# A two-layer trunk on one core: layer 0's MLP in two passes, adaLN sums held in PSUM

## The chip, the cores and the metric

The kernel runs on one core of one Trainium2 chip. The metric is the device time of one execution in microseconds (us). TensorE is PE below, with its weight loads as PEld; VectorE is DVE, ScalarE is ACT, GpSimd is POOL, and SyncE (SP) issues the DMAs.

## The reference

Two trunk layers run over 1024 sample tokens and 256 prompt tokens of width 1024, in float32. Both groups share the weights and differ in the conditioning vector. Cut to what matters here:

```python
def _trunk(x, cond, ...):
    for i in range(2):
        mod = (silu(cond) @ ada_w[i] + ada_b[i])[:, None, :]          # 1024 -> 6 * 1024
        sh1, sc1, g1, sh2, sc2, g2 = jnp.split(mod, 6, axis=-1)
        h = _rms_norm(x, norm_mix[i]) * (1.0 + sc1) + sh1
        if i == 0:
            out, s_new = _even_mixer(h, ...)     # w_in, gated chunks | retention, w_out
        else:
            out = _pool_mixer(h, od_w_pool, od_pool_scale)
        x = x + g1 * out
        h = _rms_norm(x, norm_mlp[i]) * (1.0 + sc2) + sh2
        x = x + g2 * (jnp.square(jax.nn.relu(h @ mlp_w1[i])) @ mlp_w2[i])   # 1024 -> 4096 -> 1024
    return _rms_norm(x, final_norm), states
```

## The kernel before, in words

**Layout and product.** Activations lie with channels on the 128 partitions and tokens along a row: X is 8 tiles of 128 channels by 1280 tokens, in three blocks of 512, 512 and 256 tokens. A float32 product is made of three fp32r matmuls: every operand is split into a high and a low part (names end in H and L), and `pair_pass` (L529) issues high by high, high by low and low by high. All weight products of the kernel have that line. Weights are loaded to `stage` by SP, 1 MB a unit, split by ACT (high, to `ringH`) and POOL (low, to `ringL`, L1520 or L1703), which hold two units.

**Stages in order.** Norms and input projections (to 484 us), retention (to about 540), out projection (24 output tiles, `out_update` on DVE adds each from its PSUM bank to X), layer 0's MLP (about 630 to 1525), the pool mixer (to about 1640), layer 1's MLP in two passes (to 2430), final norm and output.

**Layer 0's MLP.** 4096 hidden channels go in 16 chunks of 256. A chunk is the first matrix, squared ReLU, the second matrix, and the update of X (`update`, L1884, one DVE op a bank). The first chunk and the last are plain. In the other 14 (`mlp_fast`) the second matrix for the 1024 sample tokens is multiplied as a 2 x 2 of quarters with seven products in place of eight (Strassen-Winograd): 84 matmuls of 512 columns instead of 96. Its first matrix is plain: 96 of 512. The prompt's 256 tokens are plain in both: 96 of 256 columns a chunk.

**Layer 1's MLP.** Two passes. `plain_chunk` runs the first matrix of chunks 0 and 1; `first_pass` runs it for the other 14 with seven products of quarters, 84 matmuls of 512 columns and 48 of 256 a chunk. It needs sums of quarters of the normed input (G1 to G4, made on DVE ahead of the first product, L2338 to L2361), and sums of quarters of the weights (`qsF`, `qsH`, `qsL`, on POOL and ACT). Its results are combined on DVE and ACT (evictions s11, s22, s12 at L2390, squared ReLU B11, B22, B12 at L2396, sums T1 to T4 at L2372 to L2380) and stored to `mid_spill` in DRAM. `second_pass` runs the second matrix for pairs of chunks from pieces loaded back; `last_second` ends it. X is spilled and loaded again between the passes.

**adaLN sums.** ada_w is 1024 by 6144 a layer. It is loaded by SP three tiles of 128 outputs a batch, 1.5 MB, into `ada_st_in` or `ada_st_mlp`. `ada_part` on DVE (L1873, L1876) makes 16 multiply-adds of 128 x 384 for the 8 row tiles and the 2 conditionings, into `ada_acc_in` or `ada_acc_mlp` in SBUF. PE turns the sums with transposes into one PSUM bank (`ada_total`; L2780 in MLP 0), and DVE reduces them into `mod`. There are 27 batches. Eight run in the input projections, three in the out projection (`ADA_OUT_AT` says behind which of DVE's X updates the four parts of a batch stand, `OUT_TOTAL_AT` behind which output tile PE makes the total), and the 16 of layer 1 run one with each chunk of MLP 0. DVE is a queue in order: an X update behind an ada part waits for that part, and PE waits for its bank.

```python
ADA_OUT_AT = {2: (0, 0), 3: (0, 1), 4: (0, 2), 5: (0, 3), 9: (1, 0), 10: (1, 1), 11: (1, 2), 12: (1, 3),
              14: (2, 0), 15: (2, 1), 16: (2, 2), 17: (2, 3)}
OUT_TOTAL_AT = {8: 0, 14: 1, 19: 2}
```

**Between MLP 0 and the pool mixer.** Token tiles of X are transposed and normed (tH, tL), POOL builds the tables of the pooling bands (L1589 to L1616) in the last chunk of MLP 0, and the pool weights take a place in the rings.

Of the kernel before, what the change touches and what calls it, by code (L numbers as in the profile page):

```python
# [52 lines left out]
U_MLP = [U_OUT + N_OUT, U_OUT + N_OUT + 2 * NCH + 1]  # L53
U_ONE = U_MLP[1]
# [7 lines left out]
def two_units(ui, g):  # L62
# [7 lines left out]
ADA_IN_UNITS = {0: 0, 3: 1, 4: 2, 5: 3, 6: 4, 7: 5, 8: 6, 9: 7}  # L70
ADA_IN = ADA_BATCH * len(ADA_IN_UNITS)
ADA_L0 = NMOD - 2 * DT
ADA_OUT_TILES = [range(n, min(n + ADA_BATCH, ADA_L0)) for n in range(ADA_IN, ADA_L0, ADA_BATCH)]

ADA_OPS = 2 * DT
ADA_OUT_AT = {2: (0, 0), 3: (0, 1), 4: (0, 2), 5: (0, 3), 9: (1, 0), 10: (1, 1), 11: (1, 2), 12: (1, 3),
              14: (2, 0), 15: (2, 1), 16: (2, 2), 17: (2, 3)}
OUT_TOTAL_AT = {8: 0, 14: 1, 19: 2}
# [3 lines left out]
ADA_FIRST_AT = {9: 0, 12: 1, 15: 2, 18: 3}  # L82
BATCHES_IN = len(ADA_IN_UNITS)
BATCHES_L0 = BATCHES_IN + len(ADA_OUT_TILES)
# [15 lines left out]
LAST_MM_AT = {9: 0, 14: 1, 18: 2, 19: 3, 22: 4, 23: 5}  # L100
LAST_RS_AT = {11: 0, 16: 1, 19: 2, 21: 3}
LAST_LO_AT = {12: 0, 17: 1, 20: 2, 22: 3}
# [16 lines left out]
FAST = [range(1, NCH - 1), range(0)]  # L119
HD = DT // 2  # L120
FACTORS = {1: ("A11", "B11"), 2: ("A12", "B21"), 3: ("S4", "B22"), 4: ("A22", "T4"), 5: ("S1", "T1"), 6: ("S2", "T2"),
           7: ("S3", "T3")}
GOES_TO = {1: (0, 0), 2: (0, 0), 6: (0, 1), 5: (1, 1), 7: (1, 1), 3: (0, 1), 4: (1, 0)}
CHAIN = {6: 1, 7: 6, 4: 7, 3: 5}
FAST_SEQ = ([(1, d) for d in range(HD)] + [(2, d) for d in range(HD)]
            + [(p, d) for d0 in range(0, HD, 2) for p in (6, 5, 7, 3, 4) for d in (d0, d0 + 1)] + [("prompt", d) for d in range(DT)])
FAST_GRP = len(FAST_SEQ)
FAST_BANK = [(2, 3, 6, 1, 4, 5, 2, 3)[d] if p == "prompt" else (6, 1)[d % 2] if p in (2, 3, 5) else 2 + d for p, d in FAST_SEQ]
FAST_TILE = [(2, d) if p == "prompt" else (GOES_TO[p][1], HD * GOES_TO[p][0] + d) for p, d in FAST_SEQ]
FIRST_BANK = (0, 1, 0, 0, 0, 0)  # L130
LO_ORDER = ["B11", "B21", "T1", "T2", "B22", "T3", "T4", "p0", "p1"]
FAST_MID = len(LO_ORDER)


def earlier(seq, n):

    return max([i for i in range(n) if seq[i] == seq[n]], default=-1)


def products(l, ch):  # L140

    if not isinstance(ch, int):
# [104 lines left out]

END_NEED = [M2_END + DT * (1 + n // 4) for n in LAST_TILES]
# [9 lines left out]
def build(nc, ctx, x_prompt, x_sample, state_ret, c, c_ctx, ada_w, ada_b, norm_mix, norm_mlp, mlp_w1, mlp_w2,  # L258
# [13 lines left out]
    midH = at("midH", A_M, [P, HT, T], F32R)  # L272
    midL = at("midL", A_M + 10, [P, HT, T], F32R)
# [110 lines left out]
    r_b = [at(f"relu{i}", A_AD + 3 + 2 * i, [P, 512]) for i in range(3)]  # L384
# [55 lines left out]
    def sem(name, n=None):  # L440
# [37 lines left out]
    m1_mm, relu_ok, sqr_ok, mid_hi, mid_lo = (sem("m1_mm", 1), sem("relu_ok", 1), sem("sqr_ok", 1), sem("mid_hi", 1),  # L478
                                              sem("mid_lo", 1))
    m2_mm, m2_ev = sem("m2_mm", 2), sem("m2_ev", 2)  # L480

    s_add, s_hi, s_lo, t_full = sem("s_add", 1), sem("s_hi", 1), sem("s_lo", 1), sem("t_full", 1)
# [14 lines left out]
    def out_done(name, n):  # L497

        return mid_out[Q[name]], OUT_BASE[Q[name]] + 16 * n

    def in_done(name, n):

        return mid_in[Q[name]], IN_BASE[Q[name]] + 16 * n
# [29 lines left out]
    def ada_tiles(b):  # L533

        return (2 * DT + ADA_BATCH * b, ADA_BATCH) if b < BATCHES_IN else (2 * DT + ADA_OUT_TILES[b - BATCHES_IN][0],
                                                                          len(ADA_OUT_TILES[b - BATCHES_IN]))
# [33 lines left out]
    MID_PART = {"B11": (0, 0), "B21": (1, 0), "T1": (0, 1), "B22": (1, 1), "T2": (0, 0), "T3": (1, 0), "p0": (0, 2), "p1": (1, 2)}  # L570

    def hidden(name):

        if name == "T4":
            return ts4H[:, :], ts4L[:, :], r_b[0][:, :]
        k, tb = MID_PART[name]
        return tuple(m[:, k, cols(tb)] for m in (midH, midL, midF))

    def weight(l, name, d):

        if name[0] == "S":
            i = int(name[1]) - 1
            return tuple(m[:, i, d * P:(d + 1) * P] for m in (sumH, sumL))
        k, n0 = int(name[2]) - 1, HD * (int(name[1]) - 1)
        return tuple(r[(U_MLP[l] + 1) % 2][:, k * D + (n0 + d) * P:k * D + (n0 + d + 1) * P] for r in (ringH, ringL))
# [7 lines left out]
    def first_weight(slot, name, k):  # L593

        if name[0] == "S":
            i = int(name[1]) - 1
            return tuple(m[:, i, k * P:(k + 1) * P] for m in (qsH[0], qsL[0]))
        f, kk = int(name[1]) - 1, HD * (int(name[2]) - 1) + k
        return tuple(r[slot][:, kk * UC + f * P:kk * UC + (f + 1) * P] for r in (ringH, ringL))
# [6 lines left out]
    def second_weight(c, name, d):  # L606

        if name[0] == "S":
            i = int(name[1]) - 1
            return tuple(m[:, i, d * P:(d + 1) * P] for m in (qsH[c], qsL[c]))  # L610
        k, n0 = int(name[2]) - 1, HD * (int(name[1]) - 1)
        return tuple(r[(U_ONE + c) % 2][:, k * D + (n0 + d) * P:k * D + (n0 + d + 1) * P] for r in (ringH, ringL))

    def sum_full(s, i, c):

        return s4[:, :] if isinstance(s, int) and s == 0 and (i, c) == (4, 0) else qsF[c][:, i - 1, :]
# [5 lines left out]
    def slot_free(U):  # L622
# [308 lines left out]
    def _(act):  # L931
# [546 lines left out]
        for i in (1, 2):  # L1478
            sum1_hi(2, i)
# [1681 lines left out]
```

## Time and profile before

| | us |
|---|---|
| median of 3 runs (2449.01 to 2449.63) | 2449.06 |
| the profiled execution | 2447.29 |
| its span in the trace | 2445.4 |
| PE busy | 2396.3 |
| DVE busy | 1591.7 |
| POOL busy | 986.1 |
| ACT busy | 792.0 |

The span is what the trace covers; the execution's own time is 1.9 us longer, and that execution lies 1.8 us below the median. Times in the rows further down are from the start of the span. Of an engine's group of instructions the rows give the total time and, where engines are listed in order of time, the idle time before in brackets with the engine and line that ended it. The chain of waits follows the work back from the end, at each step to what released it. The granted clock (PEclk) is a share of TensorE's full clock.

### The profile page before, as it was taken

How to read it: one execution, taken by the hardware profiler on the slowest of the kernel's cores; microseconds unless marked ns; L12 is line 12 of the kernel's file. 1: busy time of each engine (PE TensorE's matmuls, PEld its weight loads, DVE VectorE, ACT ScalarE, POOL GpSimd, SP SyncE). 2: the span in 40 equal slices, each digit the busy share in tenths (PEclk: the TensorE clock that was granted, in tenths of full speed). 3: DMA queues.
4: the chain of work that ended last, by engine and by line, in shares of the span. 5: the costliest groups of instructions: out<-in, count | busy, mean ns of one | idle time of the engine just before them, and what ended most of it. 6: DMA issues, size and time to landing. Idle time of an engine off the chain costs nothing.

```text
span 2445.4 us, 37931 instructions
## 1 busy us (share of the span) xinstructions
PE 2396.3 (98%) x13516; PEld 2085.5 (85%) x13516; DVE 1591.7 (65%) x2600; ACT 792.0 (32%) x1234; POOL 986.1 (40%) x520
## 2 busy tenths in 40 slices
PE   8999999989999999999999999899999999999998
PEld 5988899988878888888888888878888888888887
DVE  6666842384588788877878876578333327877764
ACT  4321112151422232232223222764333334333322
POOL 0135311172033333333333333036656567876740
PEclk9999999999999999999999999999999999999999
DMA  8335433384122111212111221033343445343322
GB/s 295 121 130 155 138 130 113 123 290 143 57 70 69 60 60 60 103 60 77 60 60 60 73 90 36 18 121 125 109 147 105 144 174 215 133 146 120 120 86 87
DMA packets 156705, 274.07 MB, mean 112 GB/s; under 512 B 7716, under 2 KB 103752, under 8 KB 155720
## 3 DMA queue, kind: packets, MB, share of 16 engines
q1 hardware_dynamic: 149200, 263.22, 31.2%
q10 hardware_dynamic: 7416, 9.63, 1.4%
q8 instruction: 60, 0.98, 0.2%
q14 instruction: 29, 0.24, 0.0%
HBM read 204.66 MB, written 63.96 MB: 110 GB/s over the span
## 4 chain that ended last, share of the span: by engine, by line
PE 89%; DVE 6%; ACT 2%; issue 1%; DMA 1%; POOL 0%; SPq 0%; DVEq 0%; ACTq 0%; POOLq 0%
PE bank L529 84%; PE bank L2693 1%; PE bank L2581 1%; DMA hL_f<-in_ada_w_dram 1%; ACT yn L1140 1%; DVE X L1884 1%; DVE rst L2052 1%; PE bank L2780 0%; DVE G1L L2361 0%; DVE ada_acc_mlp L1876 0%; DVE xgm L2084 0%; DVE h1L L2091 0%; PE bank L2946 0%; PE bank L2640 0%; ACT pF L1190 0%
## 5 line engine op out<-in xcount | busy, mean ns | idle before, releaser
L1884 DVE SCALAR_TENSOR_TENSOR X<-bank,mod,X 128x512 f32<-128x512 f32 (+1 forms) x852 | 544.9, 683 | 233.1 <-PE bank L529 232.9
L529 PE MATMUL bank<-hH,ring 128*128 128x512 f32 (+1 forms) x2496 | 686.7, 357 | 0.6 <-DVE hL L2091 0.6
L1520 POOL TENSOR_TENSOR ring<-stage,ring 128x2048 fp32r<-128x2048 f32 x64 | 301.0, 4703 | 565.8 <-ACT ring L935 565.8
L529 PEld LDWEIGHTS bank<-hH,ring 128*128 128x128 f32 x2496 | 444.9, 189 | 66.7 <-DVE hL L2091 1.6
L529 PE MATMUL bank<-hL,ring 128*128 128x512 f32 (+1 forms) x1248 | 441.7, 354 | 0.0
L529 PEld LDWEIGHTS bank<-hL,ring 128*128 128x128 f32 x1248 | 236.1, 189 | 32.2
L529 PE MATMUL bank<-ring,hH 128*128 128x256 f32 (+1 forms) x1024 | 222.3, 313 | 0.4 <-DVE hL L1856 0.3
L935 ACT ACTIVATE ring<-stage 128x2048 fp32r<-128x2048 f32 x65 | 124.1, 1909 | 301.7 <-PE bank L529 289.8
L529 PE MATMUL bank<-midH,ring 128*128 128x256 f32 (+1 forms) x864 | 212.4, 327 | 4.3 <-DVE X L1884 4.3
L529 PE MATMUL bank<-h1H,ring 128*128 128x256 f32 (+1 forms) x864 | 209.5, 327 | 1.0 <-DVE h1L L2091 0.5
L529 PEld LDWEIGHTS bank<-ring,hH 128*128 128x128 f32 x1024 | 166.7, 190 | 11.5 <-DVE hL L1856 1.5
L2390 DVE TENSOR_TENSOR u<-u,bank 128x512 f32<-128x512 f32 x42 | 28.9, 688 | 213.8 <-PE bank L529 212.8
L529 PEld LDWEIGHTS bank<-midH,ring 128*128 128x128 f32 x864 | 147.0, 190 | 19.1 <-DVE X L1884 5.2
L529 PEld LDWEIGHTS bank<-h1H,ring 128*128 128x128 f32 x864 | 148.1, 190 | 17.2 <-DVE h1L L2091 1.8
L529 PE MATMUL bank<-ring,hL 128*128 128x256 f32 (+1 forms) x512 | 158.4, 309 | 0.0
L1876 DVE SCALAR_TENSOR_TENSOR ada_acc_mlp<-ada_st_mlp,sc,ada_acc_mlp 128x384 f32<-128x384 f32 (+1 forms) x266 | 147.8, 622 | 0.0
L1639 POOL TENSOR_TENSOR sumL<-sumF,sumH 128x2048 fp32r<-128x2048 f32 x14 | 64.7, 4621 | 204.3 <-DVE midF L2274 204.3
L529 PE MATMUL bank<-midL,ring 128*128 128x256 f32 (+1 forms) x432 | 141.2, 327 | 0.0
L529 PE MATMUL bank<-h1L,ring 128*128 128x256 f32 (+1 forms) x432 | 140.9, 326 | 0.0
L1703 POOL TENSOR_TENSOR ring<-stage,ring 128x1024 fp32r<-128x1024 f32 x32 | 85.2, 2674 | 58.5 <-ACT ring L1382 58.1
L529 PEld LDWEIGHTS bank<-ring,hL 128*128 128x128 f32 x512 | 97.4, 190 | 5.0
L1876 DVE SCALAR_TENSOR_TENSOR ada_acc_in<-ada_st_in,sc,ada_acc_in 128x384 f32<-128x384 f32 x112 | 99.6, 957 | 0.0
(382 smaller groups left out, 4833.8 us busy)
## 6 DMA issues: line engine op xcount, KB each, us to landing
stage<-in_mlp_w_dram SPq DMA_DIRECT2D x64, 1024.0 KB, 5.5
ada_st_mlp<-in_ada_w_dram SPq DMA_DIRECT2D x18, 1536.0 KB, 8.3
stage<-in_ev_w_in_dram SPq DMA_DIRECT2D x14, 1024.0 KB, 6.0
mid_spill<-midT SPq DMA_DIRECT2D x56, 256.0 KB, 2.2
ada_st_in<-in_ada_w_dram SPq DMA_DIRECT2D x8, 1536.0 KB, 8.3
mid_spill<-midB SPq DMA_DIRECT2D x48, 256.0 KB, 2.0
gt<-gate_spill SPq DMA_DIRECT2D x20, 256.0 KB, 3.8
x_spill<-X SPq DMA_DIRECT2D x2, 2560.0 KB, 10.5
```

The lines of the kernel that those rows point to most:

```text
L529: mm = nc.tensor.matmul(out, a, b, start=first and n == 0, stop=last and n == 2, skip_group_check=chained)
L935: nc.scalar.activation(ringH[slot][:, :], stage[:, :], ACT.Copy).then_inc(w_hi, 1)
L1140: ev = nc.scalar.activation(yn[n % 2][:, d, h, :], bank[2 + 2 * (n % 2) + d][:, h * P:(h + 1) * P], ACT.Identity, scale=rmv[n % 2][:, j, 1 ...
L1520: nc.gpsimd.tensor_tensor(ringL[slot][:, :], stage[:, :], ringH[slot][:, :].bitcast(F32), ALU.subtract).then_inc(w_lo, 1)
L1639: nc.gpsimd.tensor_tensor(sumL[:, :, :], sumF[:, :, :], sumH[:, :, :].bitcast(F32), ALU.subtract).then_inc(s_lo[l], 1)
L1703: nc.gpsimd.tensor_tensor(rows_of(ringL[slot], part), rows_of(stages[c], part), rows_of(ringH[slot], part).bitcast(F32), ALU.subtract).the ...
L1876: V.scalar_tensor_tensor(out=acc, in0=src, scalar=sc2[:, k, cond:cond + 1], in1=acc, op0=ALU.mult, op1=ALU.add).then_inc(a_acc, 1)
L1884: V.scalar_tensor_tensor(out=X[:, d, cols(t)], in0=src[:, 0:TB[t][1]], scalar=gate_ap, in1=X[:, d, cols(t)], op0=ALU.mult, op1=ALU.add).th ...
L2052: e = V.bn_stats(rst[n % 2][:, HEADS * d + h, :], bank[2 + 2 * (n % 2) + d][:, h * P:(h + 1) * P])
L2390: V.tensor_tensor(buf[:, :], buf[:, :], src[:, :], ALU.add).then_inc(m_dve, 1)
L2581: mm = nc.tensor.matmul(bank[6 + d][:, h * P:(h + 1) * P], kx[j % 2][:, d, h, :], val[:, n, h * P:(h + 1) * P], start=True, stop=True)
L2693: mm = nc.tensor.transpose(tile_pair(q, j)[:, d * P:(d + 1) * P], X[:, d, n * P:(n + 1) * P], ident)
```

## The change: MLP 0 takes the form of MLP 1, and the adaLN batches move

- **MLP 0** becomes the same code as MLP 1 (`mlp(l)` on each engine): two plain chunks, 14 first-pass chunks with seven products, `mid_spill` stores, X spilled and loaded again, seven second passes and `last_second`, whose banks are `CLOSE_BANK` for layer 0. It needs the G quarters of its input, as layer 1. The weight-quarter buffers of layer 0 lie in free parts of other tiles.
- **Layer 1's adaLN** sums: 14 of the 16 batches run one with each first-pass chunk of MLP 0. Each is loaded in two halves of 768 KB (`ada_chunk_load`, behind the stores of B11 and B21 on SP's queue), added up by DVE in two halves of 8 ops (`ada_half`) with the running sums in two PSUM banks (`chunk_bank`); only the last op of each conditioning writes SBUF (`chunk_acc`). PE turns them behind product 2 (`ada_chunk_turn`, 6 transposes) and DVE reduces them behind B11 (`ada_chunk_columns`). For the last chunk the second half falls between the passes.
- **The other two batches**, six tiles, go into the projections: nine batches in the input projections (an additional `ada_batch(1)` behind the statistics of the gates' norm), four in the out projection, in two parts each, with totals behind tiles 4, 8, 12 and 17. The loads keep their place on SP's queue.
- **The end of MLP 0**: ada work is gone from it; `LAST_MM_AT`, the order of the last token tiles, moves by a step; POOL builds the band tables behind MLP 0's last w2 low parts; the pool weights have buffers of their own (wpH, wpL), and the token tiles lie in scattered places.

```diff
-ADA_IN_UNITS = {0: 0, 3: 1, 4: 2, 5: 3, 6: 4, 7: 5, 8: 6, 9: 7}
+ADA_IN_UNITS = {0: 0, 1: 1, 3: 2, 4: 3, 5: 4, 6: 5, 7: 6, 8: 7, 9: 8}
-ADA_OUT_AT = {2: (0, 0), 3: (0, 1), 4: (0, 2), 5: (0, 3), 9: (1, 0), 10: (1, 1), 11: (1, 2), 12: (1, 3),
-OUT_TOTAL_AT = {8: 0, 14: 1, 19: 2}
+ADA_OUT_AT = {1: (0, 0), 2: (0, 1), 5: (1, 0), 6: (1, 1), 9: (2, 0), 10: (2, 1), 13: (3, 0), 14: (3, 1)}
+OUT_TOTAL_AT = {4: 0, 8: 1, 12: 2, 17: 3}
-LAST_MM_AT = {9: 0, 14: 1, 18: 2, 19: 3, 22: 4, 23: 5}
+LAST_MM_AT = {9: 0, 14: 1, 18: 2, 19: 3, 21: 4, 23: 5}
+CLOSE_BANK = [LAST_BANK[i % 4] for i in range(GRP - 4)] + [2, 3, 4, 5]
+ADA_CHUNKS = NCH - PLAIN
...
+    def chunk_bank(cond):
+
+        return (ADA_BANK, ROW_BANK)[cond][:, 0:ADA_BATCH * P]
...
+        def ada_half(n, half):
+
+            done = ADA_OPS * (BATCHES_BEFORE + n)
+            dve.wait_ge(a_raw, 16 * (BATCHES_BEFORE + 1) + 32 * n + 16 * half)
+            if half == 0:
+                dve.wait_ge(a_col, 2 * BATCHES_BEFORE + n)
+            for i in range(DT * half, DT * (half + 1)):
+                k, cond = divmod(i, 2)
+                sums = chunk_bank(cond).rearrange("p (j n) -> p j n", j=ADA_BATCH)
+                src = chunk_st[:, k - HD * half, :].rearrange("p (j n) -> p j n", j=ADA_BATCH)
+                if k == 0:
+                    V.tensor_scalar(sums, src, sc2[:, k, cond:cond + 1], None, ALU.mult).then_inc(a_acc, 1)
+                else:
+                    dve.wait_ge(a_acc, done + i - 1)
+                    V.scalar_tensor_tensor(out=sums if k < DT - 1 else chunk_acc[:, cond, :, :], in0=src, scalar=sc2[:, k, cond:cond + 1],
+                                           in1=sums, op0=ALU.mult, op1=ALU.add).then_inc(a_acc, 1)
...
+        def ada_chunk_turn(n):
+
+            pe.wait_ge(a_acc, ADA_OPS * (BATCHES_BEFORE + n) + ADA_OPS)
+            pe.wait_ge(mod_ok, 3)
+            for cond in range(2):
+                for j in range(ADA_BATCH):
+                    mm = nc.tensor.transpose(chunk_bank(cond)[:, j * P:(j + 1) * P], chunk_acc[:, cond, j, :], ident)
             mm.then_inc(a_mm, 1)
...
-        mlp(0, 0, first=True)
-        with pe.Fori(1, NCH - 1) as ch:
-            mlp_fast(0, ch)
-        mlp(0, NCH - 1, last=True)
...
+        mlp(0)
```

## Rows read from the trace of the kernel before

**Rows 1.** The page, busy time of each engine.

```profile
PE 2396.3 (98%) x13516; PEld 2085.5 (85%) x13516; DVE 1591.7 (65%) x2600; ACT 792.0 (32%) x1234; POOL 986.1 (40%) x520
```

**Rows 2.** The page, the chain that ended last, by line.

```profile
PE bank L529 84%; PE bank L2693 1%; PE bank L2581 1%; DMA hL_f<-in_ada_w_dram 1%; ACT yn L1140 1%; DVE X L1884 1%; DVE rst L2052 1%; PE bank L2780 0%; DVE G1L L2361 0%; DVE ada_acc_mlp L1876 0%; DVE xgm L2084 0%; DVE h1L L2091 0%; PE bank L2946 0%; PE bank L2640 0%; ACT pF L1190 0%
```

**Rows 3.** The chain in MLP 0: start, length, work.

```profile
888.87 46.95 PE bank L529 x252
...
941.97 46.95 PE bank L529 x252
```

**Rows 4.** The chain in layer 1's MLP and at its end.

```profile
1684.60 337.14 PE bank L529 x1800
...
2029.28 372.15 PE bank L529 x1956
2402.30 5.46 PE bank L529 x24
...
2421.34 2.87 PE bank L529 x24
```

**Rows 5.** DVE in order of time, one first-pass chunk of layer 1.

```profile
1801.01 0.69 DVE L2390 TENSOR_TENSOR u<-u,bank 128x512 f32<-128x512 f32 x1 [6.24 <-PE bank L529]
1801.73 1.81 DVE L2396 SCALAR_TENSOR_TENSOR u<-u 128x512 f32<-128x512 f32 x1
...
1817.51 0.69 DVE L2390 TENSOR_TENSOR u<-u,bank 128x512 f32<-128x512 f32 x1 [9.64 <-PE bank L529]
1818.23 1.38 DVE L2396 SCALAR_TENSOR_TENSOR midB<-u 128x512 f32<-128x512 f32 x1
1825.85 0.69 DVE L2390 TENSOR_TENSOR u<-u,bank 128x512 f32<-128x512 f32 x1 [6.23 <-PE bank L529]
```

**Rows 6.** DVE and POOL in order of time, out projection.

```profile
563.01 1.14 DVE L1873 TENSOR_SCALAR ada_acc_mlp<-ada_st_mlp,sc 128x384 f32<-128x384 f32 x2 [2.70 <-DMA ada_st_mlp<-in_ada_w_dram]
...
565.78 2.20 DVE L1876 SCALAR_TENSOR_TENSOR ada_acc_mlp<-ada_st_mlp,sc,ada_acc_mlp 128x384 f32<-128x384 f32 x4
...
602.60 3.61 DVE L1876 SCALAR_TENSOR_TENSOR ada_acc_mlp<-ada_st_mlp,sc,ada_acc_mlp 128x384 f32<-128x384 f32 x4
598.53 5.68 POOL L1520 TENSOR_TENSOR ring<-stage,ring 128x2048 fp32r<-128x2048 f32 x1 [21.06 <-ACT ring L935]
```

**Rows 7.** The page, DMA issues: KB each, us to landing.

```profile
ada_st_mlp<-in_ada_w_dram SPq DMA_DIRECT2D x18, 1536.0 KB, 8.3
```

**Rows 8.** DVE in order of time, input projections.

```profile
123.54 0.40 DVE L1964 RECIPROCAL vmv<-vmv 128x40 f32<-128x40 f32 x1 [12.02 <-ACT vmv L1107]
```

**Rows 9.** SP's queue in order of time, start of the out projection.

```profile
546.89 5.24 SPq L668 DMA_DIRECT2D ada_st_mlp<-in_ada_w_dram  x1
```

**Rows 10.** The chain in the out projection.

```profile
556.98 27.57 PE bank L529 x144
```

**Rows 11.** Windows: length, busy PE PEld DVE ACT POOL, clock, DMA share, GB/s.

```profile
1540.00:1544.00 4.00, 3.58 (x18) 3.56 (x18) 1.24 (x4) 3.67 (x8) 1.12 (x2) 0.57 0.00 0
```

**Rows 12.** Waits of PE: 630 to 730, 1630 to 1690, 1690 to 2060, 1488 to 1532.

```profile
PE bank L529 <- DVE X L1884: 2.1, 2, 1.7
...
PE bank L529 <- DVE G4L L2361: 1.9, 1, 1.9
PE bank L529 <- DVE h1L L2091: 0.5, 1, 0.5
...
PE bank L529 <- POOL ring L1703: 2.1, 1, 2.1
...
PE bank L529 <- DVE X L1884: 2.3, 1, 2.3
```

**Rows 13.** POOL in order of time: band tables, w2 low parts of layer 1.

```profile
1476.60 0.70 POOL L1589 MEMSET bandT<- 128x144 f32 x4
...
1488.75 0.10 POOL L1616 MEMSET band_edge<- 128x1 f32 x1
...
2375.40 6.36 POOL L1703 TENSOR_TENSOR ring<-stage,ring 128x1024 fp32r<-128x1024 f32 x2 [26.44 <-ACT ring L1382]
```

More of the change, by code:

```diff
@@ L568, in h_part, with tile_half, tile_rows, held_rows @@
         return (hH, hL)[part][:, d, cols(tb)]
[L570 to L585, printed above, removed]
+    def tile_half(part, n, d):
+        w = TILE_ROW[n]
+        return tile_at[n][part][:, d * P // w, d * P % w:d * P % w + P]
+    def tile_rows(n, ap):
+        return ap[:, :].rearrange("p (r w) -> p r w", w=TILE_ROW[n])
+    def held_rows(l, name, ap):
+        return ap.rearrange("p (a n) -> p a n", a=2) if l == 0 and name in ("T3", "T4") else ap
+    def held_part(l, name, m, c):
+        return m[l][name][:, 2 * c:2 * c + 2, :] if l == 0 and name in ("T3", "T4") else m[l][name][:, c, :]
+    def chunk_bank(cond):
+        return (ADA_BANK, ROW_BANK)[cond][:, 0:ADA_BATCH * P]
     def mid_at(s, name, c=None):
@@ L1305, in _ @@
+        mlp(0)
+        act.wait_ge(w_raw, raw_at(U_POOL, 1))
+        act.wait_ge(q_lo, Q_ALL)
+        nc.scalar.activation(wpH[:, :], stage[:, :], ACT.Copy).then_inc(w_hi, 1)
         act.wait_ge(band_ok, 1)
@@ L1496, in _ @@
[L1496 to L1507 removed]
+        mlp(1)
         for j in range(NT):
@@ L1774, in _ @@
[L1774 to L1781 removed]
+        mlp(1)
     @block.vector
@@ L2309, in _ @@
+        mlp(0)
+        for i, (t, d) in enumerate(BY_END):
+            update(m2_mm[0], M2_END + i + 1, m2_ev[0], bank[CLOSE_BANK[i]], mod[:, 0, 5 * DT + d, TB[t][2]:TB[t][2] + 1], t, d,
+                   (m2_ev[0], M2_END))
+            if i == 15:
+                pool_mods()
+            if i in LAST_LO_AT:
+                pool_tile_lo(LAST_LO_AT[i])
+            if i in LAST_RS_AT:
+                pool_rs(LAST_RS_AT[i])
+        pool_rs(5)
+        pool_tile_lo(5)
         for n in range(4):
@@ L2456, in _ @@
-        mid_low(0, "T2")
-        second_pass(0)
-        with dve.Fori(1, NSUP - 2) as s:
-            second_pass(s)
-        second_pass(NSUP - 2, plain=True)
-        mid_low(NSUP - 1, "T1", 3)
-        mid_low(NSUP - 1, "B22", 4)
+        mlp(1)
         for i, (t, d) in enumerate(BY_LAST):
@@ L2475, in ada_total @@
             after(pe, a_col, 2 * batch)
-            _, tiles = ada_tiles(batch)
+            _, _, tiles = ada_tiles(batch)
             for cond in range(2):
```

1829 lines of the change are left out of this document (779 added, 1050 removed).

## The prediction

> **What bounds the kernel now.** I read the page first. Its busy line [rows 1] has PE at 98% of the span, DVE at 65%; the chain [rows 2] is PE for 89%, nearly all of it the three-pass product of L529. So a time goes down here by taking matmuls away, or up by making PE wait. Next the chain inside layer 0's MLP: one fast chunk of 256 hidden channels is an unbroken run of products, from 888.87 to 941.97, 53.1 us [rows 3]. The chain in layer 1's MLP, which already runs in two passes, is one run of 1800 matmuls in the first pass and one of 1956 in the second [rows 4], 24.84 us from one s12 eviction on DVE to the next in the first pass [rows 5].
>
> The ends of the run in layer 1 give the price of a matmul: 24 of 512 columns took 5.46 us (0.2275 each), 24 of 256 took 2.87 (0.1196 each) [rows 4]. Check: a layer-0 fast chunk issues 180 of 512 (96 in the first matrix, 84 in the second), 96 of 256 and 6 transposes. The run of 252 matmuls took 46.95 us [rows 3] and the 24 left 5.46, so the transposes have 53.10 - 46.95 - 5.46 = 0.7: 180 x 0.2275 + 96 x 0.1196 + 0.7 = 53.1, as measured. A layer-1 first-pass chunk issues 84 and 48: 19.1 + 5.7 = 24.85, as measured.
>
> **The product work (removed).** Layer 0's first matrix goes from plain to seven products of quarters in 14 chunks: 12 matmuls of 512 columns fewer in each, 168 in all. 168 x 0.2275 = 38.2 us. The second matrix, the two plain chunks and all transposes keep their number (27 batches before and after). The check against rows, where two passes of the form of layer 1's stand for the new chunk: 53.10 - 0.7 - 2 x 24.84 = 2.7 a chunk, 38 in all. Term: **-38.2**.
>
> **Its cover on DVE.** PE's work only counts if DVE, ACT and POOL keep pace. In layer 1's first pass DVE is idle 6.24 and 9.64 us a chunk before its evictions [rows 5]; its own work is s12 and B12 (0.69 + 1.81) and s22 and B22 (0.69 + 1.38) as shown there, and six ops more (s11, B11, four T sums), 0.69 each like the undisturbed ones: 8.7 us, 8.8 with gaps. In layer 0 come two reduces (0.55 each) and 16 multiply-adds of 128x384. Their sums now lie in PSUM. No row shows DVE writing PSUM. Bounds: from below 0.53 us, the spacing of the SBUF form (2.20 for four [rows 6], the last of them overlapped for 0.08 by the next op); from above 1.81 us, the op with two SBUF inputs beside a busy POOL [rows 5]. I take 0.55, since the eviction that reads a bank took 0.69 for 512 columns whether its neighbour was slowed or not [rows 5], and the ada ops that slowed (3.61 for four, from 602.60, while a POOL sum ran from 598.53 to 604.21 [rows 6]) had both inputs in SBUF, which the new form has not. Sum: 8.8 + 1.1 + 16 x 0.55 = 18.7 of 24.85 us. Hidden; cost 0. It is cover no longer above (24.85 - 9.9) / 16 = 0.93 us an op. The Trainium skill (SBUF — State Buffer, "Who interferes with whom") says that a DVE instruction with at most one SBUF input doesn't contend with GpSimd; the rows above agree, and by that rule this term is 0 as well. The Trainium skill (VectorE: DVE Perf Modes, "The TRN2 errata") charges a PSUM source 62 cycles of 0.96 GHz more than an SBUF one, 65 ns; by it, as an estimate, 16 ops would take 1.0 us more a chunk, still inside the idle time, while no row here shows the difference.
>
> Placement in a chunk, T0 = the s12 eviction: first half 8.1 to 12.4, in the 9.64 us idle, so s22 isn't late; then SP issues the second 768 KB (1.5 MB land in 8.3 us [rows 7], so half in 4 to 5), which has landed at 17.5; second half 18.7 to 23.3, behind s22 and B22; s12 is due at 24.85. Queued behind this wait on DVE is only s12, with 1.5 us to spare, and PE needs its bank only a product later. SP's stage load has some 2.6 us of slack. Cost 0, up to 1 us a chunk if the load is late.
>
> **Six tiles into the projections.** In the input projections one batch more runs after bn_stats, where DVE is idle 12.02 us [rows 8] before 40 normalisations: 8.7 us fit. Cost 0; 0 to 1.
>
> In the out projection four batches run for three, and the first total goes from after output tile 8 to after tile 4. That is where I find a stall. SP's first load is issued at 546.89, behind the reload of X [rows 9], and DVE waits for it until 563.01 [rows 6]. Then 16 ops (0.53 apart) and one X update (0.66) behind the first eight: 9.2, ready at 572.2. PE reaches the new total after tile 4: tiles 3 (512 columns) and 4 (256) lie ahead from 556.98 [rows 10], 5.46 + 2.87, so 565.3. PE stands 6.9 us; behind the waiting transposes on PE are all later tiles. Before, the total stood at 556.98 + 27.57 = 584.55, so nothing waited. Later totals fit within 0 to 2 us: the second batch is loaded from 573, lands about 584 and is done at about 592, where tile 8 then ends. I take 0.5. Terms: **+6.9**, **+0.5**. The load isn't moved ahead of X's reload, so nothing excludes this; a gap between 4 (load lands sooner because fewer spills precede it) and 9 is the bound.
>
> After a gap PE's clock falls. In the pool stage, behind gaps of PE, the mean granted clock was 0.57 from 1540 to 1544 [rows 11], most of it at the lower level, 1.2 GHz. Work that would take (1 - 0.57) x 4 = 1.7 us at 2.4 GHz is lost: **+1.7** (0 to 3.4). The Trainium skill (TensorE: Matmul & The Clock Gate, Part 1) says that idleness takes the array to 1.2 GHz until activity releases it; the rows agree.
>
> **The start of MLP 0.** Before, PE waited 2.1 us for X updates behind ada ops [rows 12]. The ada ops go, and with them this wait; the norms' own waits stay. But the seven-product form needs G quarters before its first product, as in layer 1, where PE waited 1.9 for G4L and 0.5 for h1L [rows 12]; one more us, an estimate, for the last batch's two reduces ahead of them: 3.4 against 2.1. **+1.3** (-1 to +6).
>
> **Between the passes.** Layer 1 waits 2.1 us for the POOL ring [rows 12]. Layer 0 has there also the last ada half, whose load is behind the reload of X while all DMA engines are busy; DVE would end it about 2.4 us behind the product that wants its evictions. Total **+2.5** (2 to 8).
>
> **The end of MLP 0.** Before: 3.8 us without work on PE, 2.3 of them for an X update stuck behind ada ops [rows 12]. After: no ada ops there; about 1 us for w2's low parts (POOL took 6.36 us for two of them after the same point in layer 1 [rows 13]) and the tail, 1.5 before for token tiles, shorter by 0.8 at least: 3.8 to 0.8 in all. The band tables, about 12.3 us on POOL from 1476.60 [rows 13], now run behind them, ending 19.8 us after the last full pass while PE wants them at 23.3: hidden, 3.5 us of slack. **-3.0** (-4 to +3).
>
> Sum: -38.2 + 6.9 + 0.5 + 1.7 + 1.3 + 2.5 - 3.0 = -28.3. The profiled execution took 2447.29 (span 2445.4), so 2419.0 by its own time; the median of the runs is 2449.06, 1.8 higher, so **2420.8 us**, a ratio of 0.988.
>
> **Rivals.**
> A, **DVE becomes the bound** in layer 0's first pass, the case on the other side. Mechanism: the multiply-add on PSUM costs more than the SBUF form or still slows beside POOL. From 0.93 us an op each chunk lengthens by 16 times the excess; the gain of 28.3 is gone at 2.02 us a chunk, (24.85 + 2.02 - 9.9) / 16 = 1.06 us an op. At 0.90 (the four beside POOL) it is still hidden; at 1.2 us it gives 14 x 4.3 = 60 us more, 2480. For it: slow ops of DVE in [rows 5, 6] are real. Against: each has two SBUF inputs.
> B, **the out projection doesn't stall**: the load lands early, or the wait is absorbed by the queue of X updates. Then -28.3 - 6.9 - 1.7: 2412. For it: the idle of DVE before 563.01 was only 2.70 us; against: even without that idle the ops end at 569.5, 4 us late.
> C, **the seams cost more**: at the transition and at the last batch the ada load, X's reload and the spills share the DMA engines, or the band tables or low parts come late. Upper bounds above: +5.5, +4.7 and +6, not all at once: 2430 to 2437.
> D, **the first pass leaks a little**: late second halves, 1 us a chunk, 14 in all: 2435. DVE then is late for s12, shown as a wait of PE in each chunk.
>
> **Numbers.** Forecast 0.60; B 0.14; C 0.11; D 0.07; A 0.08, of which 0.02 ends between 2430 and 2444, 0.01 near no change, 0.05 above. A measurement of this kernel tells 0.2%, 4.9 us, from no change. Faster by more than that: 0.60 + 0.14 + 0.11 + 0.07 + 0.02 less 0.03 for mishaps I haven't named = 0.91; same 0.02; slower 0.07. The range must reach B below and most of C and D above: 2408 to 2436. It leaves out the worst of C, A, and a product work that is worth more than counted. The seams' bounds, B's 4 to 9 us, and the clock's 0 to 3.4 are inside.
>
> **What would show it.** Matmuls of 512 columns fewer by 168 and PE busy lower by about 38 us; fast chunks in layer 0's first pass of 24.8 to 25.2 us; no wait of PE there; the multiply-adds on PSUM at 0.53 to 0.6 us each, whatever POOL does. In the out projection a wait of PE for the ada sums near 565, of about 7 us, with a lower clock behind it. PE idle of 2 to 3 us between layer 0's passes. Against me: chunks of 26 us or more with PE waiting for DVE (A, D); no wait near 565 (B); the sum of PE's idle time from 1400 to 1500 over 5 us (C).

## The result, and the profile after

The changed kernel took 2421.93 us, median of 4 runs (2420.18 to 2423.78), where the kernel before took 2449.35 in the runs beside it: a ratio of 0.9887, 95% interval 0.987 to 0.9904. The forecast was 2420.8, a ratio of 0.988. By the profiled executions the span went from 2445.4 to 2419.0, 26.4 us less, where 28.3 were forecast.

The page of the changed kernel, busy time of each engine, answers to [rows 1]:

```profile
PE 2362.3 (98%) x13348; PEld 2057.9 (85%) x13348; DVE 1546.0 (64%) x2313; ACT 836.4 (35%) x1299; POOL 1203.2 (50%) x702
```

PE has 168 instructions fewer (13516 to 13348), exactly the matmuls counted, and is busy 34.0 us less. POOL has 217 us more work (the weight-quarter sums of a second MLP), and PE waits for it in the new stage only at the end, 0.9 us. PE's idle time rose from 49.1 to 56.7 us: 7.6 more, where the waits among the prediction's terms add up to 8.2 (6.9 + 0.5 + 1.3 + 2.5 - 3.0).

The chain of waits of the changed kernel in layer 0's first pass; columns as in [rows 3]. A chunk is 24.87 us of products and 0.66 of transposes, 25.53 in all:

```profile
792.02 0.66 PE bank L2634 x6
792.68 24.87 PE bank L529 x132
817.55 0.66 PE bank L2634 x6
818.21 24.87 PE bank L529 x132
```

DVE in such a chunk, with one op of POOL in it: the multiply-adds with their sums in PSUM run beside POOL's work. L2187 at 888.81 and 914.34 is the eviction s12 of two chunks in a row, L2095 begins a batch's first half, and the L2098 group at 908.03 begins its second:

```profile
882.51 3.23 DVE L2098 SCALAR_TENSOR_TENSOR bank<-chunk_st,sc,bank 128x384 f32<-128x384 f32 x6
883.70 3.79 POOL L1561 TENSOR_TENSOR hL<-hL_f,hH 128x512 fp32r<-128x512 f32 x3
888.81 0.69 DVE L2187 TENSOR_TENSOR u<-u,bank 128x512 f32<-128x512 f32 x1 [2.03 <-PE bank L529]
...
896.71 1.14 DVE L2095 TENSOR_SCALAR bank<-chunk_st,sc 128x384 f32<-128x384 f32 x2
...
908.03 3.23 DVE L2098 SCALAR_TENSOR_TENSOR bank<-chunk_st,sc,bank 128x384 f32<-128x384 f32 x6
...
914.34 0.69 DVE L2187 TENSOR_TENSOR u<-u,bank 128x512 f32<-128x512 f32 x1 [2.03 <-PE bank L529]
```

What PE waited for in the changed kernel, whole span (total, times, longest), the rows with adaLN and layer 0's seams in them:

```profile
PE bank L2334 <- DVE ada_acc_mlp L1787: 6.8, 1, 6.8
...
PE bank L529 <- POOL ring L1598: 3.0, 2, 2.1
...
PE bank L2634 <- DVE chunk_acc L2098: 2.3, 1, 2.3
...
PE bank L529 <- ACT u L1253: 1.7, 1, 1.7
```

The first is the stall in the out projection, forecast at 6.9. The third is the seam between layer 0's passes, forecast at 2.5. Of the second, 2.1 are layer 1's, as in [rows 12], and 0.9 are w2's low parts at the end of MLP 0, forecast at 1. The fourth lies in the first of the first-pass chunks, and no term had it. The chain there shows ACT splitting the last G quarter just before it evicts the bank that PE wants:

```profile
740.59 1.85 ACT G4H L1244 x4
...
743.45 0.58 ACT u L1253
```

The chain around the stall shows how it is made: the reload of X ahead in SP's queue (L791), the landing of the batch, and DVE's ops, then PE's transposes at 574.04, where the products before them ended at 567.2:

```profile
541.80 6.23 SPq L791
548.03 0.05 issue
548.12 16.64 DMA ada_st_mlp<-in_ada_w_dram
564.79 1.13 DVE ada_acc_mlp L1784 x2
```

And the clock behind it, windows of the changed kernel (length, busy time of PE, PEld, DVE, ACT, POOL with instructions, granted clock, DMA share, GB/s):

```profile
574.00:576.00 2.00, 1.96 (x9) 1.96 (x10) 1.04 (x2) 0.00 (x0) 0.00 (x0) 0.50 0.23 46
576.00:578.00 2.00, 2.00 (x12) 2.00 (x11) 0.00 (x0) 0.00 (x0) 0.00 (x0) 0.50 0.91 339
578.00:580.00 2.00, 2.00 (x14) 2.00 (x14) 0.00 (x0) 0.00 (x0) 0.00 (x0) 0.74 1.03 386
```

At a clock of 0.50, that is 1.2 GHz, then 0.74: 2 x 0.5 + 2 x 0.5 + 2 x 0.26 = 2.5 us of work lost, where 1.7 were forecast. The second execution of the changed kernel lost 1.7 behind the same wait, and the six variants that kept the stall 1.7 to 2.7.

### The profile page after: what moved, and what is told of

It is laid out like the page before. It is cut to its first block, busy times and chain, and to the rows that moved or that the text cites. A ratio compares the mean times of both kernels' runs of the same rounds, so it can differ in the third digit from the quotient of the medians.

```text
span 2419.0 us, 37354 instructions
## 1 busy us (share of the span) xinstructions
PE 2362.3 (98%) x13348; PEld 2057.9 (85%) x13348; DVE 1546.0 (64%) x2313; ACT 836.4 (35%) x1299; POOL 1203.2 (50%) x702
## 4 chain that ended last, share of the span: by engine, by line
PE 86%; DVE 8%; ACT 2%; DMA 1%; issue 1%; SPq 1%; POOL 0%; DVEq 0%; ACTq 0%; POOLq 0%
PE bank L529 81%; PE bank L2548 1%; DVE G1L L2158 1%; SPq L678 1%; DMA ada_st_mlp<-in_ada_w_dram 1%; PE bank L2436 1%; DMA hH_f<-in_ada_w_dram 1%; DVE G1F L2135 1%; DVE rst L1964 1%; ACT yn L1147 1%; PE bank L2844 0%; DVE G3F L2138 0%; DVE xgm L1996 0%; POOL ring L1598 0%; PE bank L2634 0%
## 5 line engine op out<-in xcount | busy, mean ns | idle before, releaser
L529 PE MATMUL bank<-hH,ring 128*128 128x256 f32 (+1 forms) x2856 | 634.4, 332 | 2.1 <-POOL ring L1598 0.9
L1795 DVE SCALAR_TENSOR_TENSOR X<-bank,mod,X 128x512 f32<-128x512 f32 (+1 forms) x576 | 373.4, 686 | 267.4 <-PE bank L529 266.1
L1447 POOL TENSOR_TENSOR ring<-stage,ring 128x2048 fp32r<-128x2048 f32 x47 | 224.6, 4778 | 295.4 <-ACT ring L942 295.4
L2187 DVE TENSOR_TENSOR u<-u,bank 128x512 f32<-128x512 f32 x84 | 57.8, 688 | 304.9 <-PE bank L529 303.0
L1598 POOL TENSOR_TENSOR ring<-stage,ring 128x1024 fp32r<-128x1024 f32 x64 | 165.2, 2597 | 112.4 <-ACT ring L1264 111.8
L529 PEld LDWEIGHTS bank<-ring,hH 128*128 128x128 f32 x1024 | 166.7, 190 | 12.2 <-DVE hL L1767 1.5
L1264 ACT ACTIVATE ring<-stage 128x1024 fp32r<-128x1024 f32 x64 | 65.8, 1056 | 219.4 <-DMA stage<-in_mlp_w_dram 181.4
L1618 POOL TENSOR_TENSOR qsL<-qsF,qsH 128x512 fp32r<-128x512 f32 x83 | 126.9, 1553 | 0.0
L1253 ACT ACTIVATE u<-bank 128x512 f32<-128x512 f32 x84 | 50.3, 599 | 196.6 <-PE bank L529 196.6
L942 ACT ACTIVATE ring<-stage 128x2048 fp32r<-128x2048 f32 x48 | 91.7, 1910 | 75.2 <-PE bank L529 71.4
L1610 POOL TENSOR_TENSOR qsF<-stage 128x512 f32<-128x512 f32 x42 | 78.3, 1876 | 56.6 <-PE bank L529 56.6
L529 PE MATMUL bank<-inpH,ring 128*128 128x256 f32 x512 | 94.5, 284 | 0.0
```

The costliest lines, as they stand in the source:

```text
L529: mm = nc.tensor.matmul(out, a, b, start=first and n == 0, stop=last and n == 2, skip_group_check=chained)
L942: nc.scalar.activation(ringH[slot][:, :], stage[:, :], ACT.Copy).then_inc(w_hi, 1)
L1253: nc.scalar.activation(dst[:, :], src[:, :], ACT.Copy).then_inc(m_act, 1)
L1264: nc.scalar.activation(rows_of(ringH[(U_MLP[l] + c) % 2], part), rows_of(stages[c], part), ACT.Copy).then_inc(w_hi, 1)
L1447: nc.gpsimd.tensor_tensor(ringL[slot][:, :], stage[:, :], ringH[slot][:, :].bitcast(F32), ALU.subtract).then_inc(w_lo, 1)
L1598: nc.gpsimd.tensor_tensor(rows_of(ringL[slot], part), rows_of(stages[c], part), rows_of(ringH[slot], part).bitcast(F32), ALU.subtract).the ...
```

## The experiments

Each starts from the changed kernel unless its edit says otherwise. Runs with several rounds are compared by their medians with its 2421.93.

**The out projection without its stall.**

```diff
-ADA_OUT_AT = {1: (0, 0), 2: (0, 1), 5: (1, 0), 6: (1, 1), 9: (2, 0), 10: (2, 1), 13: (3, 0), 14: (3, 1)}
-OUT_TOTAL_AT = {4: 0, 8: 1, 12: 2, 17: 3}
+ADA_OUT_AT = {1: (0, 0), 2: (0, 1), 7: (1, 0), 8: (1, 1), 11: (2, 0), 12: (2, 1), 15: (3, 0), 16: (3, 1)}
+OUT_TOTAL_AT = {6: 0, 10: 1, 14: 2, 19: 3}
```

> The changed kernel with its out projection's later adaLN batches and totals moved back: totals behind output tiles 6, 10, 14 and 19 in place of 4, 8, 12 and 17, and the DVE parts of batches 1 to 3 behind X updates 7/8, 11/12 and 15/16. Theory: the 6.8 us wait of PE for the ada sums near 567 goes, because DVE ends them at 574 and PE is then in tile 6, and with it the 2.5 us of half clock behind it: 9.3 us less, 2412.6 us for a kernel of 2421.9. Rival 1: the wait only moves to a later total, since the load of the next batch starts no earlier: then 0 to 4 us less. Rival 2: the half clock had another cause than this gap: then 6.8 less, and the clock near 575 is still about 0.5.

2413.79 us (2413.26 to 2414.45), ratio to before 0.9852 (0.9836 to 0.9869), 8.1 less than the changed kernel, where 9.3 were expected. The chain in this stretch of the out projection is products and transposes with nothing between them:

```profile
559.91 14.84 PE bank L529 x88
574.75 0.66 PE bank L2334 x6
575.41 19.22 PE bank L529 x96
```

The window of this kernel from 570 to 580 has PE busy throughout and the granted clock at 1.00:

```profile
570.00:580.00 10.00, 10.00 (x48) 8.32 (x48) 5.34 (x10) 1.92 (x1) 5.22 (x1) 1.00 0.47 165
```

Stall and half clock went together, and neither rival held: no later total waits. By the spans of the profiled executions the gain is 6.4: against the 9.3 taken away stand 1.3 us more of waits for pF in the pool stage (4.8 against 3.5) and 1.7 us of clock at 1650 to 1655, in layer 1's MLP.

**PE repeats 12 matmuls a chunk.**

```diff
-                    for k in range(HD):
+                    for k in [0, 1, 2, 3] * (2 if l == 0 and w_name == "A12" else 1):
```

> The changed kernel with the product A12 by B21 of layer 0's 14 first-pass chunks issued twice into its bank (the second pass of it sums on: the output of these chunks isn't the reference's): 12 matmuls of 512 columns more in each, as many as the seven-product form took away. Theory: PE is the bound in this stage with nothing to spare beside it, so the time goes up by 168 x 0.2275 = 38.2 us, to 2460.1. Rival: something else paces part of these chunks (DVE, the loads), so that matmuls there are partly free: less than 34 us.

2459.98 us (2457.38 to 2463.61), 38.05 more, against 38.2. The chain shows a chunk's products at 27.59 us where they were 24.87, which is 38.1 us in 14 chunks:

```profile
769.29 27.59 PE bank L529 x144
```

168 matmuls cost their full price in this stage, so the ones that the change removed were worth what was counted.

**The sums in SBUF.**

```diff
-                sums = chunk_bank(cond).rearrange("p (j n) -> p j n", j=ADA_BATCH)
+                sums = chunk_acc[:, cond, :, :]
```

> The changed kernel with the running ada sums of layer 0's first pass in SBUF (chunk_acc) in place of PSUM, so each multiply-add has two SBUF inputs; all else as it is. Theory: beside POOL's sums these ops slow down, as the sum u<-u does (1.8 for 0.7 us): the 8 of the second half take 6 to 9 us in place of 4.3, and the 8 of the first half 5 to 7; DVE's work goes from 18.3 to 22 to 26 us of the chunk's 25.5, so PE begins to wait or just doesn't: 2422 to 2450 us. Rival A (PSUM as the place of the sums is worth nothing here): the ops stay at 0.54 us each and the time at 2422.

2489.59 us (2482.53 to 2494.48), 67.7 more; ratio to before 1.0166 (1.0139 to 1.0192). Against before the whole change is then a loss. The changed kernel's DVE, groups of instructions from 744 to 1060 (busy us, mean ns):

```profile
L2098 DVE SCALAR_TENSOR_TENSOR bank<-chunk_st,sc,bank 128x384 f32<-128x384 f32 x150 | 80.9, 611 | 4.0 <-DMA chunk_st<-in_ada_w_dram 4.0
```

The groups with the sums in SBUF, from 770 to 1070 (the first and the third are those of the adaLN sums):

```profile
L2098 DVE SCALAR_TENSOR_TENSOR chunk_acc<-chunk_st,sc,chunk_acc 128x384 f32<-128x384 f32 x147 | 157.6, 1140 | 34.7 <-DMA chunk_st<-in_ada_w_dram 34.7
L2187 DVE TENSOR_TENSOR u<-u,bank 128x512 f32<-128x512 f32 x32 | 21.7, 677 | 0.0
L2095 DVE TENSOR_SCALAR chunk_acc<-chunk_st,sc 128x384 f32<-128x384 f32 x20 | 20.3, 1057 | 1.1
```

The multiply-add went from 611 to 1140 ns in the mean (lengths of single records, which overlap: on PSUM the next one starts after 0.525). DVE's eviction, which reads a bank, stayed at 677, and DVE is never idle before it: it was late each time. DVE in order of time shows the slowing, first in an op with one SBUF input and an SBUF output (the median of the 28 of its kind is 0.42 us), then in six multiply-adds; eight others took less:

```profile
895.67 4.77 DVE L2095 TENSOR_SCALAR chunk_acc<-chunk_st,sc 128x384 f32<-128x384 f32 x1
900.36 8.33 DVE L2098 SCALAR_TENSOR_TENSOR chunk_acc<-chunk_st,sc,chunk_acc 128x384 f32<-128x384 f32 x6
...
914.21 5.36 DVE L2098 SCALAR_TENSOR_TENSOR chunk_acc<-chunk_st,sc,chunk_acc 128x384 f32<-128x384 f32 x8 [4.19 <-DMA chunk_st<-in_ada_w_dram]
```

POOL in order of time has one op of the same length over the first, was busy beside the six up to 907.75, and was idle from there to 917.36:

```profile
895.48 4.75 POOL L1447 TENSOR_TENSOR ring<-stage,ring 128x2048 fp32r<-128x2048 f32 x1
...
903.11 4.64 POOL L1561 TENSOR_TENSOR hL<-hL_f,hH 128x512 fp32r<-128x512 f32 x3
...
917.36 1.79 POOL L1561 TENSOR_TENSOR hL<-s,hH 128x512 fp32r<-128x512 f32 x1 [9.61 <-ACT hH L1249]
```

The direction was as expected and the size was not: I had 0 to 28 us. The 34.7 us in which DVE waited for `chunk_st` were in no theory: a late first half makes the second half's load late, since both use one buffer. PE waited 41.3 us for DVE's sums of u and 6.5 more at the seam (8.8 for 2.3); the clock behind these gaps took about 14 more. The Trainium skill (SBUF — State Buffer, "Who interferes with whom") says that a tensor_scalar between SBUF tensors can take the port pair that DVE shares with GpSimd, and an op with two SBUF inputs contends with GpSimd's reads; the rows above agree, and by it the PSUM form escapes, as its 611 ns show. The prediction gave this rule without the case of the tensor_scalar.

**How much cover DVE has.** 12 and 24 more multiply-adds a chunk:

```diff
                     dve.wait_ge(a_acc, done + i - 1)
+                    for _ in range(1 if k not in (0, DT - 1) else 0):
+                        V.scalar_tensor_tensor(out=chunk_acc[:, cond, :, :], in0=src, scalar=sc2[:, k, cond:cond + 1], in1=sums,
+                                               op0=ALU.mult, op1=ALU.add)
```

> The changed kernel with 12 multiply-adds more for DVE in every first-pass chunk of layer 0 (6 in each half; they write what the last ops of the half-sums overwrite, so the output stays). Theory: DVE had 7.2 us idle of a chunk's 25.5, 12 x 0.53 = 6.4 fit, and PE needs s12 only behind two products of the next chunk: no change, 2422 (0 to 10 us more, because the second half's load is issued 3.2 us later). Rival A in its weaker form (any delay on DVE reaches PE at once): +3 us a chunk, 45 us more.

2448.26 us (2444.72 to 2450.68), 26.3 more, where 0 to 10 were expected: a miss. The added ops cost 0.525 us each, as counted, so DVE's work is not over a chunk's time. DVE in order of time shows what is:

```profile
882.78 1.14 DVE L2095 TENSOR_SCALAR bank<-chunk_st,sc 128x384 f32<-128x384 f32 x2
...
890.84 0.75 DVE L2196 SCALAR_TENSOR_TENSOR midB<-u 128x512 f32<-128x512 f32 x1
895.25 0.62 DVE L2099 SCALAR_TENSOR_TENSOR chunk_acc<-chunk_st,sc,bank 128x384 f32<-128x384 f32 x1 [3.66 <-DMA chunk_st<-in_ada_w_dram]
...
902.61 0.68 DVE L2190 TENSOR_TENSOR u<-u,bank 128x512 f32<-128x512 f32 x1
...
909.58 1.14 DVE L2095 TENSOR_SCALAR bank<-chunk_st,sc 128x384 f32<-128x384 f32 x2
```

From one first half to the next are 26.80 us: the half 7.35 (to 890.13), the load that waits for it 5.12 (to 895.25), the second half 7.36 (to 902.61), then s12 to B11 5.85 and the reduces 1.12. It is a loop through one staging buffer, longer than PE's 25.53. The excess of 1.27 us a chunk is 17.8 in 14 chunks. The rest lies at the ends of the stage: PE waited 7.7 us at the seam in place of 2.3 and 2.4 for u in the first chunks, and the clock behind these waits took about 3.

> The same with 24 more a chunk, each waiting for the op before. Theory: DVE's work is then 18.3 + 24 x 0.53 = 31 us or more of 25.5, DVE is the bound of the stage, 5.6 us a chunk or more in 14 chunks: +78 us at least, 2500, PE waiting for DVE in each chunk. Rival: the cover is larger than I count, less than 40 us more.

Here each multiply-add of the kernel waits for the kernel's one before, and all but the last two of a batch have two more ahead of them:

```diff
-                    dve.wait_ge(a_acc, done + i - 1)
+                    dve.wait_ge(a_acc, done + i)
+                    for c in (cond, 1 - cond) if k < DT - 1 else ():
+                        V.scalar_tensor_tensor(out=chunk_acc[:, c, :, :], in0=src, ...)
```

2555.45 us (2548.75 to 2556.26), 133.5 more. DVE's work alone would give 78 or a little more, the least that was expected; the loop gives 11.3 + 5.4 + 11.4 + 5.5 + 1.1 = 34.7 us a chunk, 14 x (34.7 - 25.5) = 129. PE waited 70.6 us for `chunk_acc` and 27.9 for DVE's sums of u; the clock after these gaps took about 31.

**The 12 ops without the load in the loop.**

```diff
                 mid_store(s, c, "B11", "B11")
-                if l == 0 and not (closing(s) and c == 1):
-                    ada_chunk_load(ch - PLAIN, 1)
...
-            dve.wait_ge(a_raw, 16 * (BATCHES_BEFORE + 1) + 32 * n + 16 * half)
+            dve.wait_ge(a_raw, 16 * (BATCHES_BEFORE + 1) + 16 * n)
```

> The kernel with 12 multiply-adds more a chunk, but without the load of the second half of layer 1's adaLN weights in the chunks: the second half uses the first half's data again (layer 1's modulation isn't the reference's). Before it, that kernel had taken 26.3 us more than the changed one, though DVE's work fits into a chunk. Theory now: what set its chunk was a loop through the one staging buffer: half, load of 5.1 us that waits for it, half, then s12 to B11 (5.85) and the reduces (1.1): 7.35 + 5.1 + 7.35 + 5.85 + 1.1 = 26.8, as its trace shows. With the load away the loop is 7.35 + 2.1 (s22, B22) + 7.35 + 5.85 + 1.1 = 23.8, under the 25.5 of PE: the time returns to 2422 (2418 to 2426), and DVE never waits for a DMA. Rival: the added ops as such delay PE (their PSUM traffic, or any delay of s12): 2435 to 2448 stays.

2428.89 us (2426.99 to 2430.73): 19.4 of the 26.3 us are gone. The chain shows PE unbroken at its old chunk, with as many added ops as the kernel with 12:

```profile
872.17 24.87 PE bank L529 x132
897.04 0.66 PE bank L2633 x6
897.70 24.87 PE bank L529 x132
```

What is left, 7 us, lies at the ends of the stage: PE's wait at the seam is 5.5 us in place of 2.3, one of 2.4 for u stands in the first chunks, and the clock behind the two took about 4 us of work (the sum is that of one execution, whose span is 8.4 longer). In the chunks between, the loop through the load was the cause, and the ops as such cost nothing. The edit also takes 768 KB of traffic a chunk away, but what the kernel with 12 ops shows is DVE waiting for this very load, 42.2 us from 780 to 1060, and here that wait is gone.

**The seam, twice.** First PE's turn of the last sums moved behind the first product of the second pass:

```diff
                 for p in SEQ2:
+                    if l == 0 and isinstance(s, int) and s == 0 and p == "2":
+                        ada_chunk_turn(ADA_CHUNKS - 1)
...
-                ada_chunk_turn(ADA_CHUNKS - 1)
             second_pass(0)
```

> The changed kernel with one edit at the seam between layer 0's passes: PE turns the last chunk's ada sums behind the first product of the second pass, not ahead of it. Theory: the 2.3 us wait of PE for chunk_acc near 1093 is the order of DVE's queue (two low parts of pieces ahead of 8 multiply-adds), and the first product, 5.5 us, needs nothing of it: the wait goes and no other of more than 0.5 us takes its place, PE idle in this stretch falls from 2.3 to under 0.5. Rival: PE then stands for the low part of B11 or for the POOL ring, as layer 1 does (2.1 us) at the same place: idle stays at 1.5 to 2.3.

One run gave 2425.28. What PE waited for from 1060 to 1130:

```profile
PE bank L529 <- DVE X L1795: 2.6, 1, 2.6
PE bank L529 <- DVE u L2187: 1.5, 1, 1.5
```

4.1 us in place of 2.3: the rival held in kind, though PE stood for s12 and the X updates and not for B11 or a ring. Behind them the granted clock was 0.93 from 1100 to 1110 and 0.90 from 1110 to 1120, where the changed kernel has 1.00 in both. Then the same with s12 and B12 ahead of the last 8 multiply-adds on DVE, and the late totals:

```diff
-                    if l == 0:
-                        ada_half(ch - PLAIN, 1)
                 total("s12", u2, bank[2], "3", "u2")
                 relu_squared("B12", u2)
+                if l == 0 and closing(s) and c == 1:
+                    ada_half(ch - PLAIN, 1)
```

> The kernel with the late totals of the out projection, and at the seam between layer 0's passes s12 and B12 on DVE ahead of the last 8 multiply-adds, and PE's turn of them behind the first product of the second pass. Theory: PE's 2.3 us wait at the seam was work in DVE's queue ahead of s12, which this puts behind it; the first product starts at once and the turn waits 1.7 us or less: 1 to 2 us less than the late totals alone, 2412. Rival: DVE as such is the bound at the seam (it has some 13 us of work from the end of the last product on before its first X update), so the wait only moves, as it did when the turn alone was moved (PE idle 4.1 in place of 2.3): 2413 to 2416.

2413.82 us (2412.06 to 2415.85), beside 2413.79 for the late totals alone: no change, as the rival said, where 2412 was the theory. At the seam PE waited 1.2 us for the POOL ring and 2.5 for X. The wait moves with the order of DVE's queue and doesn't go.

**Both kernels once more, for the clock in the pool stage.**

> The kernel before once more, for a second profile. In the first one the pool stage's granted clock cost 5.1 us (the sum of one less the clock over its stretches); in five profiles of the changed kernel and its variants, whose pool stage is the same code on the same data but for the token tiles' places, it cost 7.5 to 10.8. Theory: the phase in which the gaps fall differs from execution to execution, so that this second profile can give any value from 3 to 10. Rival: the changed kernel's pool stage loses more as such: again 5 us here.

> The changed kernel once more, for a second profile. Theory: the waits repeat (6.8 us in the out projection, 2.3 at the seam), while the clock's loss in the pool stage differs: 8.6 us in the first profile, 5 to 12 in six variants with the same pool stage, 5.1 and 3.4 in two profiles of the kernel before. Rival: it is 8.6 again, a property of the kernel and not of the execution.

The pool stage in the first execution of before, as a window of 110 us; the clock is the last figure but two:

```profile
1530.00:1640.00 110.00, 99.52 (x634) 87.86 (x633) 71.69 (x110) 76.21 (x129) 17.07 (x14) 0.95 0.19 70
```

The same window in its second execution:

```profile
1530.00:1640.00 110.00, 99.63 (x646) 88.38 (x645) 70.94 (x109) 76.48 (x131) 16.84 (x13) 0.97 0.19 70
```

The changed kernel's first execution, 28 us earlier as the stage is:

```profile
1502.00:1612.00 110.00, 101.19 (x627) 90.12 (x625) 69.81 (x106) 72.99 (x124) 16.86 (x13) 0.92 0.19 70
```

And its second:

```profile
1500.00:1610.00 110.00, 100.62 (x630) 89.45 (x630) 70.50 (x107) 73.92 (x126) 16.86 (x13) 0.94 0.19 70
```

Lost to the clock, by windows of 2 us over the whole stage: 5.1 and 3.4 us before; 8.5 and 6.8 after. In the eight variants, all with the changed pool stage, it was 5.1 to 12.0, in four of them 8.5 or 8.6. It differs between executions of one kernel, as the theory said. The ten profiles with the changed stage have a mean of 8.5, and only one, 5.1 in the seam order, is as low as the higher of the two of before. That suggests a part that belongs to the kernel; no run shows where it would come from. The second execution of the changed kernel took 2418.06 us and repeated its waits (6.8 and 2.3).

## Why the prediction was right, by its own steps

The time was forecast to 1.1 us, and that is closer than the terms were: what the sum left out (3.9 us) was partly cancelled by terms that came out smaller and by PE being busy less than counted. That part was luck.

**The product work**, -38.2: shown, by the count of instructions and by the 38.05 us that as many matmuls cost when put back. One sign was off: I had named chunks of 24.8 to 25.2 us, and they are 25.53, since the transposes, which the sum rightly left alone, are in them.

**Its cover on DVE**, 0: the multiply-adds on PSUM took 0.54 us (3.23 for six) where 0.55 was taken, with POOL busy beside them, and PE never waited in the chunks between. The places held too: the first half lay 7.9 to 12.2 us behind s12 and the second from 19.2 on, where 8.1 to 12.4 and 18.7 were worked out. The value was right and one step of it was wrong: the threshold of 0.93 us an op, (24.85 - 9.9) / 16, came from adding up DVE's work. The runs showed that the loop through the staging buffer closes first: 16 ops, the load of 5.1 and 5.85 + 1.1 us. Against a chunk of 25.53 (the 0.66 of transposes belonged in it too) that is (25.53 - 12.1) / 16 = 0.84 us an op. I had taken "placement in a chunk" for a matter of up to 1 us where the load is late; 12 ops more made it 26 us.

**The out projection**, +6.9 and +0.5: measured 6.8 and 0. The start of DVE's ops was 564.79 by the trace after, where 563.01 was taken from before, and PE came 1.9 us later as well, so the difference held. The bound from 4 to 9 was not needed.

**The clock behind it**, +1.7: measured 2.5 in the first execution and 1.7 in the second. The row that it was taken from lies behind other gaps than this one, so its exact value was chance; the range of 0 to 3.4 holds all eight profiles with the stall. Wait and clock together are 9.3; the late totals won 8.1 of them back in the medians.

**The start of MLP 0**, +1.3: by the windows PE was idle 3.97 us from 630 to 730 before and 2.53 + 2.31 from 630 to 1040 after, +0.9. The size was near and the step behind it was wrong: PE didn't wait for a G quarter at all (the 2.0 for G4L are layer 1's). It waited 1.7 for ACT's eviction of u and 0.6 for its midp, in place of the 2.1 for X updates. By the chain above, the last G quarter cost its time through ACT's queue, where G4H stands ahead of that eviction. **Between the passes**, +2.5: 2.3. **The end of MLP 0**, -3.0: idle 3.8 us before, 0.9 after, -3.0 with rounding, and the band tables were hidden: POOL had them at 1460.0, and PE's first product with them stands at 1468.19.

**What no term had.** PE was 1.8 us later at 484, and 1.2 of them are waits for the first adaLN loads (3.3 us against 2.1). In the second executions these waits are 2.3 and 0.9: they differ by about 1 us from execution to execution, and the changed kernel has the longer ones both times, though the two kernels do the same there. I can't place it. The pool stage, taken as unchanged, lost 3.4 us more to the clock and had 1.3 less idle time. Together with 0.8 more of the clock behind the stall and 1.2 less in the other waits that is 3.5 us too many. Against it PE was busy 34.0 us less, where -38.2 and the clock's 2.5 + 3.4 give 32.3: 1.7 us that nothing here explains. With them the -28.3 of the forecast becomes -26.5, and the span's is -26.4.

**Rivals.** A (DVE the bound) didn't happen, and is near: with the sums in SBUF the kernel is 1.7% slower than before. Its price had been worked out at 1.2 us an op as 60 us; the SBUF sums had a mean of 1.14, for which the same sum gives 46, and cost 68: the loop through the load and the clock behind the gaps were not in it. B was wrong about the kernel and right about what it is worth: 2412 without the stall, measured 2413.79. C and D stayed away: seams +0.9, +2.3 and -3.0, no wait in a chunk.

## What to carry to other kernels

Where an engine in the shade of another shares one staging buffer with a load, its reserve isn't its idle time: add up the loop from the first use through the load that waits for it and back, and compare that with the period. A sum that DVE must keep beside a busy GpSimd was better kept in PSUM here, and a batch that is moved earlier in one engine's order is only as early as its load. Before a hand-written order is moved up by some tiles, work out when the data lands; here the totals two tiles later were worth 8 us of a change worth 27.

## What the runs showed of the hardware that I had not expected

PE can stay at the lower clock for long with work at hand. After a gap of about 1 us in 1508 to 1510, the changed kernel ran 10 us at 1.2 GHz in its pool stage, with PE busy all the time:

```profile
1511.00:1521.00 10.00, 9.83 (x46) 9.75 (x47) 2.97 (x6) 8.30 (x16) 2.87 (x4) 0.50 0.00 0
```

Its second execution ran about 7 us so, and the comparable stretch of before 3.4 us behind gaps of its own ([rows 11]). What decides it wasn't tried. And a DVE multiply-add whose sum lies in PSUM, input and output, took the same 0.54 us as the one in SBUF with POOL quiet (2.20 for four, [rows 6]): the trace shows no price for PSUM in this op.
